# First units of five products begun in the tails of the stages ahead, with four changes of order, in a two-block transformer kernel on one core

## The chip, the core and the metric

The kernel runs on 1 core of a Trainium2 chip as one program. The metric is the device time of one execution in microseconds, from all inputs in device memory to the output there. TensorE (PE) multiplies, VectorE (DVE) and ScalarE (ACT) do the elementwise work, GpSimd (POOL) adds some squares and moves rows, and SyncE (SP) issues the loads.

## The reference, cut to what matters

All of it is fp32, for 512 tokens (plus 256 context tokens in layer 0), width 1024. Two layers of a first block are followed by a second block.

```
def first_block(...):
    for l in range(2):
        ...
        h = h + mx[2] * (yx @ w_out[l])
        h = h + mx[5] * conv_ffn(modulate(rmsnorm(h, norm2_g[l]), mx[3], mx[4]), w_up[l], conv_w[l], conv_b[l], w_down[l])
        ...
    return rmsnorm(h, final_g)

def conv_ffn(h, w_up, conv_w, conv_b, w_down):      # 1024 -> 2 x 2816 -> 1024
    u = h @ w_up
    ...
    return (jax.nn.silu(a) * b) @ w_down
```

The second block normalises the result twice (`final_g`, then `mix_g`), multiplies by `w_in_2`, mixes (latent attention of 8 heads and a "hyena" long convolution with filters computed in the kernel), multiplies by an output matrix, attends to 256 memory tokens with 4 heads of 256 (`w_mq`, `w_mkv`, `w_mo`) and ends in a mixture of 32 experts.

```
def _mem_xattn(hx, hm, w_mq, w_mkv, w_mo):
    q = (hx @ w_mq).reshape(B, S, MEM_HEADS, MEM_HEAD_DIM)
    k, v = jnp.split(hm @ w_mkv, 2, axis=-1)
    ...
    return o @ w_mo
```

## The kernel before, in words

**Stages.** The program is a chain of stages (`with self.stage()`). Each gives every engine a hand-written list of work, with semaphores between the lists. At the end of a stage all engines wait for each other; the profile shows that wait as PEq L784.

**Products in three passes.** A large product (`project`) is made of units: one unit is 128 output rows (a PSUM area), summed over 8 or 22 tiles of 128 input rows. Both operands are split in a high part (rounded, made by ACT, L824, L505 or L608) and a low part (value minus high, made by DVE, L859, L509 or L612). One tile costs three matmuls: high weight by low input, high by high, low by high. A unit of 8 tiles is 24 matmuls, all at L953.

**Weight strips.** Weights come in strips of up to 2048 columns through a ring of 3 slots (`ring`). A strip must be split before PE uses it; its high part goes to one of two areas in turn, so strip s+2 can be split only when PE is done with strip s. `split_order` sets the order of the splits on ACT and DVE alike: first strip 0 (unless the stage ahead has split it, `following_strip` or `split_ahead`), then the tiles that are not ready, then for each unit the strips whose area is free, the norm work (`deferred.on_vector`, `on_scalar`, at unit 0) and the eviction of the unit (`take`). With `early=k` strip 1 is split ahead of tile k; without it, strip 1 comes behind all tiles. `tiles_ahead` says how many tiles the stage ahead has split already.

**The places that the change touches**, in order of time:
1. Down projection of layer 0 (`ffn_down`, no tile ahead): 22 tiles of 768 tokens, two strips of 1408 columns for a unit, strip 1 from tile 11 on.
2. Down projection of layer 1 (9 tiles ahead, 512 tokens). SP first loads the inputs of the hyena filters (`load_hyena_inputs`), and PE stops ahead of unit 1 for them (`FilterFeatures.on_tensor`, L466).
3. `second_projection`, behind `hyena_filters`: 16 units of 8 tiles, 5 tiles ahead (`PAIRED_AHEAD`). Units 0 and 1 use strip 0, units 2 and 3 strip 1, units 4 and 5 strip 2. `PairNorm` adds squares on ACT (L523) and DVE (L547), PE sums them over partitions (L533, in `before`), DVE and ACT form the two inverse roots (L549 to L555), and only then DVE evicts units 0 and 1 (L2291) and splits strip 2.
4. `latent_attention`: 32 steps u (a head's quarter): scores (L1081), maximum (L1149), exponential (L1196), scaling (L1155, L1156), transposition (L1123), copy (L1234), and every 8 steps the values (L1092). At u = 4 ACT splits two whole strips of the next product and at u = 5 DVE does (`high_ahead`, `low_ahead`). Its last sum of squares is L1071.
5. `mixed_projection`: 16 half units. Three of its tiles come from the hyena part and are ready early.
6. `memory_attention`'s product: 24 units of 256 and 512 columns, `MemoryNorm`, 8 memory tiles ahead.
7. The memory attention itself: 16 steps with the same loop, two strips split at u = 4 and 5; copies of values are L1169.
8. `output_projection` behind it: 8 units, 6 of 8 tiles ahead.

## Time and profile before

| | us |
|---|---|
| median of 3 runs | 2773.83 |
| lowest, highest | 2773.24, 2775.17 |
| the profiled execution, its own time | 2779.62 |
| span of its instructions | 2777.8 |
| PE busy in it | 2487.8 (90%) |
| DVE busy | 1375.2 (50%) |
| ACT busy | 868.5 (31%) |
| mean granted TensorE clock | 0.949 |

The profiled execution is one run with the profiler on. Its span starts at the first instruction, and all stretches below are in microseconds of that span. A granted clock of 1.00 is 2.4 GHz and 0.50 is 1.2 GHz; a value between them is a stretch that has some of both.

### The profile page before, as it was taken

How to read it: one execution, taken by the hardware profiler on the slowest of the kernel's cores; microseconds unless marked ns; L12 is line 12 of the kernel's file. 1: busy time of each engine (PE TensorE's matmuls, PEld its weight loads, DVE VectorE, ACT ScalarE, POOL GpSimd, SP SyncE). 2: the span in 40 equal slices, each digit the busy share in tenths (PEclk: the TensorE clock that was granted, in tenths of full speed). 3: DMA queues.
4: the chain of work that ended last, by engine and by line, in shares of the span. 5: the costliest groups of instructions: out<-in, count | busy, mean ns of one | idle time of the engine just before them, and what ended most of it. 6: DMA issues, size and time to landing. Idle time of an engine off the chain costs nothing. (4 is left out here: it accounts for less than half of the span.)

```text
span 2777.8 us, 34833 instructions
## 1 busy us (share of the span) xinstructions
PE 2487.8 (90%) x14602; PEld 1933.5 (70%) x14602; DVE 1375.2 (50%) x2185; ACT 868.5 (31%) x1385; POOL 251.7 (9%) x183
## 2 busy tenths in 40 slices
PE   7997988999998998997889999998977889898976
PEld 5885657888887787995669998764733368573322
DVE  4324554566667214325647777347565645423213
ACT  3222433332324113223444334233424642311001
POOL 0002520000000000003500000000042020011112
PEclk9998989999999999997989999999988999988999
DMA  5114731111111112115612223320201013348997
GB/s 240 61 54 106 269 128 46 46 61 61 63 69 38 53 63 82 61 69 142 224 46 92 92 92 117 111 82 31 87 0 54 0 61 137 121 188 326 421 421 292
DMA packets 58555, 326.88 MB, mean 118 GB/s; under 512 B 8157, under 2 KB 14429, under 8 KB 26461
## 3 DMA queue, kind: packets, MB, share of 16 engines
q1 hardware_dynamic: 45358, 302.76, 29.4%
q0 software_dynamic: 5696, 12.59, 1.2%
q10 hardware_dynamic: 7344, 9.28, 1.0%
q8 instruction: 117, 1.92, 0.3%
q14 instruction: 40, 0.33, 0.0%
HBM read 317.26 MB, written 12.58 MB: 119 GB/s over the span
## 5 line engine op out<-in xcount | busy, mean ns | idle before, releaser
L953 PE MATMUL ps<-work_rounded,ring_rounded 128*128 128x512 f32 (+1 forms) x2016 | 537.0, 354 | 19.1 <-DVE work_rounded L397 10.6
L953 PE MATMUL ps<-xn_rounded,ring_rounded 128*128 128x512 f32 (+2 forms) x2304 | 541.8, 347 | 0.0
L2003 PE MATMUL ps<-xn_rounded,ring_rounded 128*128 128x258 f32 (+2 forms) x2816 | 535.1, 312 | 0.0
L2003 PEld LDWEIGHTS ps<-xn_rounded,ring_rounded 128*128 128x128 f32 x2816 | 414.6, 191 | 31.2
L953 PEld LDWEIGHTS ps<-xn_rounded,ring_rounded 128*128 128x128 f32 x2304 | 373.4, 191 | 57.6 <-issue 0.2
L953 PEld LDWEIGHTS ps<-work_rounded,ring_rounded 128*128 128x128 f32 x2016 | 336.5, 192 | 76.3 <-DVE work_rounded L397 11.8
L953 PE MATMUL ps<-big_rounded,ring_rounded 128*128 128x512 f32 (+1 forms) x1200 | 326.3, 364 | 45.0 <-DVE big_rounded L859 25.0
L859 DVE TENSOR_TENSOR ring_rounded<-ring,ring_rounded 128x2048 fp32r<-128x2048 f32 (+2 forms) x94 | 189.1, 2015 | 266.5 <-ACT ring_rounded L824 266.5
L2003 PE MATMUL ps<-work_rounded,ring_rounded 128*128 128x256 f32 (+1 forms) x1232 | 280.2, 309 | 9.0 <-PEq L784 4.8
L953 PEld LDWEIGHTS ps<-big_rounded,ring_rounded 128*128 128x128 f32 x1200 | 203.4, 196 | 84.8 <-DVE ring_rounded L859 21.4
L824 ACT ACTIVATE ring_rounded<-ring 128x2048 fp32r<-128x2048 f32 (+2 forms) x94 | 158.2, 1687 | 314.7 <-PE ps L953 298.3
L2003 PEld LDWEIGHTS ps<-work_rounded,ring_rounded 128*128 128x128 f32 x1232 | 191.9, 191 | 21.5 <-issue 10.6
L2052 DVE TENSOR_TENSOR ring_rounded<-ring,ring_rounded 128x1024 fp32r<-128x1024 f32 x84 | 103.0, 1226 | 171.4 <-ACT ring_rounded L2017 171.4
L2017 ACT ACTIVATE ring_rounded<-ring 128x1024 fp32r<-128x1024 f32 x84 | 89.0, 1060 | 205.8 <-PE ps L2003 205.8
L2022 ACT ACTIVATE work<-work,small 128x512 f32<-128x512 f32 (+1 forms) x132 | 81.5, 649 | 203.0 <-DVE work L2059 203.0
L1313 ACT ACTIVATE big<-big,small 128x512 f32<-128x512 f32 (+1 forms) x81 | 47.0, 624 | 254.0 <-DVE big L1309 154.0
L1303 DVE COPY small<-ps 128x2 f32<-128x2 f32 x46 | 7.3, 159 | 176.9 <-PE ps L953 176.6
L3320 PE MATMUL ps<-big,work 128*64 128x512 f32 x352 | 80.4, 604 | 15.1 <-DMA big<-in_experts 13.8
L1339 POOL MEMSET work<- 128x792 f32 x2 | 1.5, 758 | 1015.4 <-DMA work<-in_pool 1015.4
L2070 DVE SCALAR_TENSOR_TENSOR work<-work,vec 128x769 f32<-128x769 f32 (+1 forms) x88 | 78.0, 887 | 3.1
L2069 DVE SCALAR_TENSOR_TENSOR work<-work,vec 128x769 f32<-128x769 f32 (+1 forms) x88 | 78.0, 887 | 3.1
L3343 ACT ACTIVATE work<-ps,small 128x256 f32<-128x256 f32 x16 | 7.6, 476 | 221.3 <-PE ps L3320 221.3
(420 smaller groups left out, 3125.4 us busy)
## 6 DMA issues: line engine op xcount, KB each, us to landing
ring<-in_stream SPq DMA_DIRECT2D x141, 1024.0 KB, 4.8
big<-in_experts SPq DMA_DIRECT2D x44, 1024.0 KB, 26.0
ring<-in_stream SPq DMA_DIRECT2D x32, 704.0 KB, 4.0
ring<-in_experts SPq DMA_DIRECT2D x22, 1024.0 KB, 27.3
xn<-in_experts SPq DMA_DIRECT2D x15, 1024.0 KB, 28.4
work<-in_experts SPq DMA_DIRECT2D x15, 1024.0 KB, 28.7
big<-in_first_modulation SPq DMA_DIRECT2D x8, 1024.0 KB, 14.1
work<-in_bias ACTq DMA_DIRECT2D x24, 256.0 KB, 3.9
```

Source lines behind the costliest of these rows:

```text
L824: return act.activation(self.rounded(high), value, ACT.Copy)
L859: return dve.tensor_tensor(self.rounded(value), value, self.rounded(high).bitcast(F32), ALU.subtract)
L953: mm = pe.matmul(out[:, a - u.first:b - u.first], lhs, rhs, start=j == 0 and n == 0 and not u.onto, stop=j == terms - 1 and n == len(passe ...
L1313: act.activation(px[:, m, a:z], px[:, m, a:z], ACT.Identity, bias=bias[:, m, s:s + 1])
L2003: mm = pe.matmul(out[:, a:b], ws[:, k, :], x[k][:, a - base:b - base], start=k == 0 and n == 0, stop=k == KT - 1 and n == 2)
L2017: act.activation(high_w[c], half(i, c)[0], ACT.Copy).then_inc(strip_high.up(), 1)
L2022: ins = act.activation(u[:, i % 2, c, o:o + b - a], u[:, i % 2, c, o:o + b - a], ACT.Identity, bias=bias[:, i % 2, c, s:s + 1])
L2052: dve.tensor_tensor(low_part, value, high_w[c].bitcast(F32), ALU.subtract).then_inc(strip_low.up(), 1)
L2069: settle(dve, dve.scalar_tensor_tensor(out=cc, in0=uu[:, 0:n], scalar=cw(0, t), in1=cc, op0=ALU.mult, op1=ALU.add), vstep)
L2070: dve.scalar_tensor_tensor(out=cc, in0=uu[:, 2:2 + n], scalar=cw(2, t), in1=cc, op0=ALU.mult, op1=ALU.add).then_inc(convolved.up(), 1)
L3320: mm = pe.matmul(b.bank(2)[r, :], self.rows_t[:, k, r], self.gu[s][:, k, :], start=k == 0, stop=k == KT - 1)
L3343: act.activation(self.silu_t, b.bank(2)[:, 0:256], ACT.Silu, scale=b.slot_scale[:, 0, n:n + 1]).then_inc(self.silued, 1)
```

## The change

Four changes of order:
- `PairNorm.before`: PE sums the squares ahead of unit 4 instead of unit 2 (place 3).
- In both attentions the two whole-strip splits become four half-strip splits, on ACT at u = 4, 6, 8, 10 and on DVE at u = 5, 7, 9, 11 (places 4 and 7).
- `ffn_down` gets `early=8` in layer 0 and `early=10` in layer 1 (places 1 and 2).
- The last two tiles of the memory attention's output are split at the end of the attention instead of at the start of the output projection (place 8).

And `begin_unit`: in the tails of the stages ahead, PE issues the first matmuls of the next product. These are 9 tiles of unit 0 (27 matmuls) at place 2, 5 tiles (15) at place 3, 3 tiles of units 0 to 3 (36) at place 5, 7 tiles of 256 columns (21) at place 6, and 6 tiles of units 0 and 1 (36) at place 8. `project` leaves them out then (`begun`). No matmul is added or removed.

```
     def before(self, pe, i):
-        if i == 2:
+        if i == 4:
             pe.wait_ge(b.sig("squares_added").sem, b.sig("squares_added").at(2 * KT - 2))
...
+    def begin_unit(self, pe, out, strip, weight, sources):
+        slot = self.ring[:, strip % RING * STRIP:strip % RING * STRIP + WIDTH[strip]]
+        high_w, low_w = [self.rounded(self.high_of(strip))], [self.rounded(slot)]
+        for j, (low, high) in enumerate(sources):
+            for n, (w, x) in enumerate(((high_w, low), (high_w, high), (low_w, high))):
+                pe.matmul(out, weight(w, j), self.rounded(x), start=j == 0 and n == 0, stop=False)
...
-                    for j, tile in enumerate(u.tiles):
+                    for j, tile in list(enumerate(u.tiles))[begun.get(i, 0):]:
...
+                if begin:
+                    begin(pe)
...
                 values(heads - 1)
+                if begin:
+                    pe.wait_ge(exped.sem, exped.at(units))
+                    begin(pe, 0)
                 if normed_pairs:
                     sum_pair(heads // 2 - 1)
+                if begin:
+                    begin(pe, 1)
...
-                    if u == 5:
-                        self.low_ahead(dve, views)
...
+                    if u in (5, 7, 9, 11):
+                        halves_low((u - 5) // 2)
+                    next_lows(u)
                 store(heads - 1)
+                next_lows(units)
...
-                    if u == 4:
-                        self.high_ahead(act, views)
+                    if u in (4, 6, 8, 10):
+                        halves_high((u - 4) // 2)
+                    next_highs(u)
...
+                if tiles_ahead:
+                    pe.wait_ge(next_low.sem, next_low.at(tiles_ahead + 1))
+                    self.begin_unit(pe, self.ps[:, 0:width], len(self.freed_at), self.down_weight, down_sources[0:tiles_ahead])
...
-        self.project(units, 2 * KT, finish, banks_each=2, sources=sources, tiles_ahead=tiles_ahead,
+        self.project(units, 2 * KT, finish, banks_each=2, sources=sources, tiles_ahead=tiles_ahead, early=10 if last else 8, begun={0: tiles_ahead},
...
+                pe.wait_ge(next_low.sem, next_low.at(PAIRED_AHEAD))
+                pe.wait_ge(taken.sem, taken.at(5))
+                self.begin_unit(pe, self.bank(0), len(self.freed_at), halves(0), norm.rooms[0:PAIRED_AHEAD])
...
-        self.project(units, 4, finish, sources=rooms, deferred=OutputNorm(self, rooms, w[:, 7168:7680]), add=square, gpsimd=add_squares,
-                     following_strip=True, after=after, tiles_ahead=4)
+        self.project(units, 4, finish, sources=rooms, deferred=OutputNorm(self, rooms, w[:, 7168:7680]), add=square, gpsimd=add_squares,
+                     following_strip=True, after=after, tiles_ahead=4, begin=begin, begun={m: 3 for m in range(4)})
...
-        self.project(units, 12, finish, sources=norm.rooms, deferred=norm, early=KT, tiles_ahead=KT)
+        self.project(units, 12, finish, sources=norm.rooms, deferred=norm, early=KT, tiles_ahead=KT, begun={0: KT - 1})
...
-            next_tiles=[(6 + 4 * (m // 2), 2 * (m // 2) + 2, o[:, m, :], self.output_high[m]) for m in range(6)])
+            next_tiles=[(6 + 4 * (m // 2) if m < 6 else 16, 2 * (m // 2) + 2, o[:, m, :], self.output_high[m]) for m in range(KT)], begin=begin)
...
-                               tiles_ahead=6, rooms=self.output_high)
+                               tiles_ahead=KT, rooms=self.output_high, begun={0: 6, 1: 6})
```

How it moves instructions at three of the places. First DVE at place 1, from the start of layer 0's down projection (`big_rounded` is a tile's low part, `ring_rounded` a strip's; a row with x8 stands for eight of them). Before:

```order
L972 UNCONDITIONAL_BRANCH [waits barrier_Pool_Activation_PE_DVE_SP_release]
L859 TENSOR_TENSOR ring_rounded<-ring,ring_rounded 128x1408 [waits strip_high]
L859 TENSOR_TENSOR big_rounded<-big,xn_rounded 128x768 [waits tile_high] x8
L859 TENSOR_TENSOR big_rounded<-big,work_rounded 128x768 [waits tile_high] x14
L859 TENSOR_TENSOR ring_rounded<-ring,ring_rounded 128x1408 [waits strip_high] x2
L2121 SCALAR_TENSOR_TENSOR h<-ps,mods,h 128x512 [waits product_done]
```

With the change:

```order
L984 UNCONDITIONAL_BRANCH [waits barrier_Pool_Activation_PE_DVE_SP_release]
L859 TENSOR_TENSOR ring_rounded<-ring,ring_rounded 128x1408 [waits strip_high]
L859 TENSOR_TENSOR big_rounded<-big,xn_rounded 128x768 [waits tile_high] x8
L859 TENSOR_TENSOR ring_rounded<-ring,ring_rounded 128x1408 [waits strip_high]
L859 TENSOR_TENSOR big_rounded<-big,work_rounded 128x768 [waits tile_high] x14
L859 TENSOR_TENSOR ring_rounded<-ring,ring_rounded 128x1408 [waits strip_high]
L2164 SCALAR_TENSOR_TENSOR h<-ps,mods,h 128x512 [waits product_done]
```

Strip 1 moved from behind tile 21 to ahead of tile 8.

Next PE at place 3, around the sum of squares L533. Before, with the last matmuls of unit 1 ahead of it and the first of unit 2 behind it:

```order
L953 MATMUL ps<-work_rounded,ring_rounded 128x512
L953 MATMUL ps<-xn_rounded,ring_rounded 128x512 x2
L533 MATMUL ps<-xn,base 128x512 [waits squares_added]
L533 MATMUL ps<-xn,base 128x512
L953 MATMUL ps<-work_rounded,ring_rounded 128x512 [waits strip_low]
```

With the change; 96x512 is unit 3, and the `strip_low` behind the sum is that of strip 2:

```order
L963 MATMUL ps<-work_rounded,ring_rounded 96x512
L963 MATMUL ps<-xn_rounded,ring_rounded 96x512 x2
L533 MATMUL ps<-xn,base 128x512 [waits squares_added]
L533 MATMUL ps<-xn,base 128x512
L963 MATMUL ps<-work_rounded,ring_rounded 128x512 [waits strip_low]
```

The sum moved behind two more units. DVE's order at the same place is that of before (the eviction, L2291 before, is now L2337):

```order
L547 TENSOR_TENSOR xn<-xn 128x512 [waits squares_added,squared] x12
L549 TENSOR_SCALAR work<-ps 128x512 [waits summed]
L550 TENSOR_SCALAR xn<-work 128x512 [waits varied]
L551 SCALAR_TENSOR_TENSOR xn<-ps,xn 128x512 [waits vector_step]
L553 RECIPROCAL xn<-xn 128x512 [waits rooted,varied]
L555 RECIPROCAL work<-work 128x512 [waits rooted,vector_step]
L2337 TENSOR_TENSOR big<-ps,xn 128x512 [waits product_done,vector_step]
L2337 TENSOR_TENSOR big<-ps,xn 128x512 [waits product_done]
L859 TENSOR_TENSOR ring_rounded<-ring,ring_rounded 128x2048 [waits strip_high]
```

Nothing moved there: `summed` is what PE's L533 sends, and the last row splits strip 2.

Last DVE at place 4, at steps 5 to 7 of the latent attention. Before:

```order
L1156 TENSOR_SCALAR work<-work,small 128x512 [waits vector_step]
L1149 TENSOR_REDUCE small<-ps 128x1 [waits scored]
L1150 TENSOR_SCALAR small<-small 128x1 [waits vector_step]
L859 TENSOR_TENSOR ring_rounded<-ring,ring_rounded 128x2048 [waits strip_high] x2
L1155 RECIPROCAL small<-small 128x1 [waits exponentials]
L1156 TENSOR_SCALAR work<-work,small 128x512 [waits vector_step]
```

With the change:

```order
L1168 TENSOR_SCALAR small<-small 128x1 [waits vector_step]
L859 TENSOR_TENSOR ring_rounded<-ring,ring_rounded 128x1024 [waits strip_high]
L1173 RECIPROCAL small<-small 128x1 [waits exponentials]
L1174 TENSOR_SCALAR work<-work,small 128x512 [waits vector_step]
L1167 TENSOR_REDUCE small<-ps 128x1 [waits scored]
L1168 TENSOR_SCALAR small<-small 128x1 [waits vector_step]
L1173 RECIPROCAL small<-small 128x1 [waits exponentials]
L1174 TENSOR_SCALAR work<-work,small 128x512 [waits vector_step]
L1167 TENSOR_REDUCE small<-ps 128x1 [waits scored]
L1168 TENSOR_SCALAR small<-small 128x1 [waits vector_step]
L859 TENSOR_TENSOR ring_rounded<-ring,ring_rounded 128x1024 [waits strip_high]
L1173 RECIPROCAL small<-small 128x1 [waits exponentials]
```

Two whole strips in a row became one half every second step.

## Rows read from the trace of the kernel before

**Rows 1.** The page, part 1: busy time of each engine, share, instructions.

```profile
PE 2487.8 (90%) x14602; PEld 1933.5 (70%) x14602; DVE 1375.2 (50%) x2185; ACT 868.5 (31%) x1385; POOL 251.7 (9%) x183
```

**Rows 2.** PE's waits, whole span: total us, times, longest us.

```profile
PE ps L953 <- DVE big_rounded L859: 25.0, 3, 12.1
PE ps L1123 <- DVE work L1156: 24.9, 21, 6.0
PE ps L953 <- PEq L784: 15.1, 5, 6.0
```

**Rows 3.** PE by stretches: start:end length, busy (x matmuls), clock, DMA share, GB/s.

```profile
912.74:918.37 5.63, 5.63 (x17) 0.50 0.00 0
...
1718.54:1724.58 6.04, 0.01 (x1) 0.66 0.34 119
...
2155.50:2158.58 3.08, 2.93 (x12) 1.00 0.00 0
2167.51:2171.97 4.46, 4.46 (x13) 0.60 0.00 0
2234.43:2238.09 3.66, 1.13 (x3) 1.00 0.00 0
2238.09:2283.11 45.02, 45.02 (x192) 1.00 0.20 71
2301.32:2304.15 2.83, 0.00 (x0) 1.00 0.64 197
2304.15:2307.59 3.44, 3.44 (x16) 0.50 0.35 143
2418.28:2419.42 1.14, 1.14 (x6) 1.00 0.00 0
2406.42:2408.60 2.18, 2.18 (x6) 0.50 0.00 0
2432.99:2434.11 1.12, 0.00 (x1) 1.00 0.00 0
```

**Rows 4.** The page, part 5: splits of 1024 columns; busy us, mean ns.

```profile
L2052 DVE TENSOR_TENSOR ring_rounded<-ring,ring_rounded 128x1024 fp32r<-128x1024 f32 x84 | 103.0, 1226 | 171.4 <-ACT ring_rounded L2017 171.4
L2017 ACT ACTIVATE ring_rounded<-ring 128x1024 fp32r<-128x1024 f32 x84 | 89.0, 1060 | 205.8 <-PE ps L2003 205.8
```

**Rows 5.** Timeline at place 1: start, length, instruction, [idle before <- releaser].

```profile
898.91 12.25 DVE L859 TENSOR_TENSOR big_rounded<-big,work_rounded 128x768 fp32r<-128x768 f32 x14
...
903.74 0.51 PE L953 MATMUL ps<-big_rounded,ring_rounded 128*128 128x512 f32 x2
...
912.74 1.01 PE L953 MATMUL ps<-big_rounded,ring_rounded 128*128 128x512 f32 x2 [5.70 <-DVE ring_rounded L859]
```

**Rows 6.** Timeline at place 2: the splits, and the stop for the hyena inputs.

```profile
1725.21 7.32 DVE L859 TENSOR_TENSOR big_rounded<-big,xn_rounded 128x512 fp32r<-128x512 f32 x12 [1.02 <-ACT xn_rounded L824]
...
1742.92 1.07 PE L466 MATMUL ps<-work,vec 33*64 33x512 f32 x2
```

**Rows 7.** DMA traffic of 1724 to 1744, in 40 slices of 0.5 us.

```profile
GB/s 0 0 12 153 351 243 360 246 246 197 229 295 475 377 492 754 98 737 246 590 442 344 541 246 590 197 737 246 541 101 438 383 383 101 23 34 11 0 0 34
```

**Rows 8.** Timeline at place 3: bank 0 read, the sum, the chain behind it.

```profile
1901.63 0.68 DVE L2248 COPY big<-ps 1x512 f32<-1x512 f32 x1 [3.18 <-PE ps L2209]
...
1920.23 1.98 PE L533 MATMUL ps<-xn,base 128*128 128x512 f32 x4 [2.30 <-DVE xn L547]
...
1935.00 2.29 DVE L859 TENSOR_TENSOR ring_rounded<-ring,ring_rounded 128x2048 fp32r<-128x2048 f32 x1 [2.03 <-ACT ring_rounded L824]
...
1937.35 0.79 PE L953 MATMUL ps<-work_rounded,ring_rounded 128*128 128x512 f32 x1 [4.02 <-DVE ring_rounded L859]
```

**Rows 9.** Timeline at places 4 and 7: the whole-strip splits and what PE waited.

```profile
2162.37 4.50 DVE L859 TENSOR_TENSOR ring_rounded<-ring,ring_rounded 128x2048 fp32r<-128x2048 f32 x2 [1.35 <-ACT ring_rounded L824]
...
2406.42 0.69 PE L1123 MATMUL ps<-base,work 128*128 128x128 f32 x2 [5.68 <-DVE work L1156]
...
2418.28 0.44 PE L1123 MATMUL ps<-base,work 128*128 128x128 f32 x2 [1.28 <-DVE work L1156]
```

More of the change, by code:

```diff
@@ L878, in project @@
     def project(self, units, strips, finish, sources, banks_each=1, prefetch=None, deferred=None, add=None, gpsimd=None,
-                early=None, following_strip=False, loads=None, following_halves=False, after=None, beside=None, tiles_ahead=0):
+                early=None, following_strip=False, loads=None, following_halves=False, after=None, beside=None, tiles_ahead=0,
+                begun={}, begin=None):
         first = len(self.freed_at)
@@ L1197, in exponentials, with next_highs, halves_high @@
                                    accum_out=stat[:, 2, b:b + 1]).then_inc(exped.up(), 1)
+                def next_highs(u):
+                    for at_unit, outputs, value, high in next_tiles:
+                        if u == at_unit:
+                            act.wait_ge(stored.sem, stored.at(outputs))
+                            self.split_high(act, value, high).then_inc(next_high.up(), 1)
+                def halves_high(part):
+                    for n, value, high in views[part // 2:part // 2 + 1]:
+                        r = slice(part % 2 * 1024, part % 2 * 1024 + value.shape[1] // 2)
+                        self.strip(act, n)
+                        self.split_high(act, value[:, r], high[:, r]).then_inc(strip_high.up(), 1)
                 def square_pair(p):
@@ L2115, in ffn_down @@
         g, segments = self.g, self.gates(l, 5, need_ctx)
-        units = [Unit([2 * m, 2 * m + 1], lambda w, j: w[j // 11].rearrange("p (k c) -> p k c", k=FT // 2)[:, j % 11, :], range(FT), P, width)
-                 for m in range(KT)]
+        units = [Unit([2 * m, 2 * m + 1], self.down_weight, range(FT), P, width) for m in range(KT)]
         def finish(eng, i, ps):
@@ L2631, in rows, with begin @@
             return slice(64 * (h % 2), 64 * (h % 2) + 64)
+        next_low, strip = self.sig("next_low"), len(self.freed_at)
+        def begin(pe, part):
+            if part == 0:
+                pe.wait_ge(next_low.sem, next_low.at(4))
+            for m in (2 * part, 2 * part + 1):
+                self.begin_unit(pe, self.bank(m), strip, self.half_strip(m), [(mix[:, 4 + i, :], self.hyena_high()[i]) for i in range(3)])
         self.attention(
@@ L2722, in finish, with begin @@
             return dve.tensor_tensor(dst[i], ps, memory_rstd if i < KT else stream_rstd, ALU.mult)
-        self.project(units, 12, finish, sources=norm.rooms, deferred=norm, early=KT, tiles_ahead=KT)
+        self.project(units, 12, finish, sources=norm.rooms, deferred=norm, early=KT, tiles_ahead=KT, begun={0: KT - 1})
         self.output_high = tiles_in(S, w[:, 3072:7168])
         self.sparse = SparseExperts(self)
+        next_low, strip = self.sig("next_low"), len(self.freed_at)
+        def begin(pe, part):
+            if part == 0:
+                pe.wait_ge(next_low.sem, next_low.at(6))
+            self.begin_unit(pe, self.bank(2 * part), strip, halves(part), [(o[:, m, :], self.output_high[m]) for m in range(6)])
         self.attention(
```

56 lines of the change are left out of this document (34 added, 22 removed).

## The prediction

> **What bounds the kernel now.** I read the busy times first: PE is busy 90% of the span [rows 1], so what can be won is PE's idle time and the time in which it runs at 1.2 GHz. PE's waits come next [rows 2]: the three longest entries add up to 65 us, and most single waits are of 1 to 12 us at a stage's border or inside an attention. Then I went to each place that the change touches and asked which engine ends the wait there. Three prices recur. At 2.4 GHz 192 matmuls of 512 columns take 45.02 us [rows 3], so 0.2345 us each, 0.70 us for a tile and 5.63 us for a unit of 8 tiles. Behind the waits of 5.7 us at place 1 and 2.83 us at place 6 PE came back at 1.2 GHz, for 5.63 and 3.44 us, both at clock 0.50 [rows 3]; such a stretch costs half its length. And a split of 1024 columns takes DVE 1.23 us and ACT 1.06 [rows 4].
>
> **Place 1, down projection of layer 0 (early=8).** PE waits 5.70 us at 912.74 for strip 1 [rows 5], since DVE split 22 tiles first, the last 14 of them in 12.25 us. Now strip 1 comes ahead of tile 8. It has 1408 columns, so it takes at most 1.7 us. That delays tile 8, the first of the 14 in [rows 5], from 898.91 + 0.88 = 899.8 to 901.5. PE needs it at 903.74 [rows 5], so 2.2 us of cover are left, and the later tiles come every 0.88 us, quicker than PE uses them (three matmuls of 512 columns and three of 256, so 1.05 us). The wait goes whole, and with it the 5.63 us at 1.2 GHz behind it [rows 3], worth 2.8. Next late is nothing: DVE is then ahead of PE. Sum: 5.7 + 2.8 = **+8.5 us** (between 5.7, if the clock fell all the same, and 8.5).
>
> **Place 2, down projection of layer 1 (9 tiles begun, early=10).** PE idled 6.04 us at the border [rows 3] while DVE ended the convolution. The 27 matmuls take 6.3 us at 2.4 GHz and fill that. PE then is the last at the border, by some 0.7 us. Behind it tile 9 comes first, strip 1 (1.7 us) next, then tiles 10 to 21 at DVE's 0.61 us each (7.32 us for 12 [rows 6]), faster than PE's 0.70. PE would end unit 0 near 1738, against 1742.92, where L466 starts [rows 6]. But L466 waits for the hyena inputs, four loads of 4.9 MB together, that SP issues at the border. Traffic stays high until 1740.5 [rows 7]; the last 0.7 MB are a strip queued behind them, so they land between 1739.3 and 1740.9, and 0.7 us later with the border. PE goes on between 1740.0 and 1741.6. The transfer, hidden before, takes half of the gain. Sum: 1742.9 - 1740.5 = **+2.4 us** (1.3 to 2.9). A stretch at 1.2 GHz in unit 0 would be lost in the same wait.
>
> **Place 3, second projection (15 begun, sum ahead of unit 4).** This is where I expect a loss. The wait of 4.02 us at 1937.35 ends with DVE's split of strip 2 [rows 8], and that split stands on DVE behind everything that follows the sum: three steps, two roots on ACT, two reciprocals, the evictions of units 0 and 1, then ACT's high part. From the start of the sum (1920.23) to PE's next unit (1937.35) the chain takes 17.1 us [rows 8]. Before, PE did units 2 and 3 (11.3 us) beside it and waited 4.02. With the change units 2 and 3 stand ahead of the sum, nothing of PE's is left beside the chain, and unit 4 needs its end. When does the sum start? The 15 begun matmuls (3.5 us) can start when DVE has read bank 0, at 1902.3 [rows 8], and end at 1905.9; the border moves some 1.2 us later, tiles 5 to 7 follow until about 1910.0, three units (16.9) until 1926.9. The chain ends at 1926.9 + 17.1 = 1944.0, against 1937.35: **-6.7 us** (-5 to -10; the upper end if PE runs the units ahead of the sum at 1.2 GHz for two stretches of 3.4 us). The wait of 2.30 us in [rows 8] is gone, and one of some 15 us comes. Queued behind DVE's wait for the sum are the evictions and strip 2. The begun matmuls alone bring nothing here: with the sum ahead of unit 2 it would still wait for the squares, which start at the border.
>
> **Places 4 and 7, halves in the attentions.** In the latent attention PE waited 6.0 us while DVE split two strips in 4.50 us [rows 9], and then ran two steps in 4.46 us that take 3.08 elsewhere [rows 3]: 5.9 more than usual, plus 1.4 for the clock, 7.3. Now each half is 1.23 us on DVE and 1.06 on ACT. A step is a loop through DVE, ACT and PE with about no slack (PE is busy 2.93 of the 3.08 us of two steps [rows 3], and waits for DVE's scaling each time, 21 waits in [rows 2]), so DVE's 4 x 1.23 = 4.9 all shows. The first half also waits for ACT (0.5 us), and the second stands ahead of a copy that PE needs (0.6). That is 6.0 to 6.3, so **+1.0 us** (-1.8, if ACT's four add in full, 9.1, to +7.3, if all is hidden). In the memory attention PE waited 5.68 us [rows 9], of which 1.28 is the wait at the same step of the next head [rows 9], and one step took 2.18 us for 1.14 [rows 3]: 5.4 in all. The same halves cost 4.9 plus about 1.1, where tiles are split at the same steps: **-0.6 us** (-3.7 to +5.4).
> The first row is 4.50 us for two whole strips, and four halves are 4.9. The Trainium skill, in Perfetto Trace Analysis, Optimizing Scalar/DVE Operations, says that breaking up instructions may allow work to be completed sooner where these engines aren't saturated but cause bubbles on others. By that rule the halves vanish in the idle time; the rows on the loop speak against it, and the case is a rival below.
>
> **Place 5, tail of the latent attention (36 begun).** PE idled 3.66 - 1.13 = 2.5 us [rows 3] around the last sum. The 36 matmuls (8.4 us) cover that; what stays is the border itself, about 0.4 us. DVE's and ACT's work of the next stage starts 6 us later, but PE has 60 of its first 96 matmuls left (14 us); DVE needs about as long for strip 2. **+2.0 us** (1.3 to 2.2).
>
> **Place 6, memory products (21 begun).** They fill idle time ahead of the border, but PE waits again at 2301.32 for 2.83 us [rows 3], and that wait ends with DVE's list (strip 1, eight tiles, three reciprocals, two evictions, strip 2), which starts at the border whatever PE has done. Nothing is won. The wait grows to some 7 us, and the 3.44 us at 1.2 GHz behind it [rows 3] may get longer: **-0.4 us** (-1.7 to 0).
>
> **Place 8, output projection (36 begun, two tiles split earlier).** PE idled 1.12 us [rows 3] and now about 0.4: **+0.7 us** (0.3 to 0.7). The two splits lie beside the begun matmuls.
>
> **Sum.** 8.5 + 2.4 - 6.7 + 1.0 - 0.6 + 2.0 - 0.4 + 0.7 = +6.9 us. The profiled execution took 2779.62 us, 1.8 more than its span and 5.8 more than the median of the three runs. 2779.6 - 6.9 = 2772.7, and less 5.8 it is 2766.9: I say **2767 us**. The loads of the experts at the end start from PE's progress and shift with it.
>
> **Rivals.**
> (a) Slower. At both attentions ACT's half adds to DVE's, and the repeated gaps keep the clock at 1.2 GHz through steps 5 to 12. Each then costs 9.1 us, plus 8 steps at 4.46 for 3.08 per two (5.5) in one and some 4 in the other: 14.6 and 13.1 us against 7.3 and 5.4. That is 15 us worse, and 0.4 less gain: 2767 + 15.4 = 2782; with only one of the two, near 2775. It decides from the granted clock there falling to 0.5 for more than 5 us. For it speaks the 0.60 at 2167.51 [rows 3]; against it that each gap would be under 2.6 us, and that the clock is 1.00 right behind the 1.28 us wait in the memory attention [rows 3].
> (b) The late sum costs nothing, because strip 2 is not behind the chain as I read it. Then place 3 wins the 2.30 us instead of losing 6.7: 2758. Against it: the row ahead of 1937.35 is that split.
> (c) The halves vanish in idle time, by the rule above: 12.7 us won for my 0.4, so 2754.7. DVE has idle time only while PE runs the values.
> (d) The begun matmuls and early strips move work and little else: place 1 gives only 5.7, place 2 1.3, place 3 costs 9: 6.9 - 2.8 - 1.1 - 2.3 = 0.7, so 2773.
>
> **How the numbers follow.** My forecast, 2763 to 2770, has a chance of 0.52; (d) and what lies between, 2770 to 2775, 0.30; (a) 0.08; (b) 0.06; (c) 0.04. The range reaches from 2760 to 2774. A measurement can tell about 0.2%, 5.5 us, from no change. The border of 2768.3 cuts my forecast: faster 0.37 of its 0.52, plus (b), (c) and a part of (d) (0.09), is 0.56; slower is most of (a) and a little of (d), 0.07; the rest, 0.37, is within.
>
> **What the changed profile would show.** Right: at place 1 no wait of PE between 907 and 919 and clock 1.00 there. At place 2 PE busy through the border and a new wait of about 2 us ahead of L466. At place 3 L533 without a wait of its own, and behind it PE waiting some 15 us for L859. In the attentions four waits of 1 to 2.5 us for one of 6. At place 6 a wait of about 7 us for 2.8. Wrong: a wait under 8 us behind L533, a clock of 0.50 through the attentions, or strip 1 still late at place 1.

## The result, and the profile after

The changed kernel is slower. Its four runs took 2781.85, 2790.98, 2791.21 and 2790.30 us (median 2790.64), against a median of 2774.5 for before beside them; the ratio is 1.0045, with a 95% interval of 1.0033 to 1.0057. Measured again on another chip (11 runs, below) it was 1.0035 (1.0020 to 1.0051). These ratios, here and below, are estimates over all runs and not quotients of the medians. The forecast was 2767 us.

The profiled execution of the changed kernel is the one of 2781.85 us. Its busy times (the page, part 1) differ from [rows 1] by hardly anything, since no product was added:

```profile
PE 2486.1 (89%) x14602; PEld 1927.9 (69%) x14602; DVE 1376.2 (50%) x2189; ACT 869.3 (31%) x1389; POOL 252.0 (9%) x183
```

So I cut both traces at the stages' borders. The columns of the view by stretches are start:end, length, PE busy (x matmuls), granted clock, DMA share, GB/s. Before, from the border ahead of the hyena filters' stage (`hyena_filters`, between places 2 and 3), then that stage, place 3, place 4, place 5, place 6, place 7 and place 8:

```profile
1852.12:1853.30 1.18, 0.01 (x1) 1.00 0.35 56
1853.30:1901.59 48.29, 45.60 (x104) 1.00 0.05 21
1901.59:2006.46 104.87, 94.93 (x388) 0.95 0.18 63
2148.04:2234.43 86.39, 68.80 (x262) 0.92 0.05 19
2234.43:2283.11 48.68, 46.15 (x194) 1.00 0.19 65
2283.11:2384.86 101.75, 95.68 (x585) 0.97 0.36 125
2385.98:2432.99 47.01, 35.24 (x128) 0.93 0.32 133
2432.99:2479.13 46.14, 45.02 (x193) 1.00 0.33 134
```

The same view of the changed kernel: first place 1 without any wait, then the same eight stretches, with the low clock inside the filters' stage as a row of its own:

```profile
891.59:1078.26 186.67, 186.67 (x1056) 0.99 0.17 62
...
1835.17:1836.35 1.18, 0.01 (x1) 1.00 0.41 76
1836.35:1896.08 59.73, 58.86 (x104) 0.77 0.04 16
1838.47:1865.78 27.31, 27.31 (x33) 0.50 0.03 11
...
1896.08:2008.78 112.70, 94.77 (x388) 0.91 0.16 59
2150.14:2235.97 85.83, 70.75 (x263) 0.92 0.05 20
2235.97:2282.40 46.43, 46.02 (x197) 1.00 0.19 68
2282.40:2385.30 102.90, 95.30 (x585) 0.95 0.35 123
2386.41:2437.07 50.66, 38.41 (x129) 0.90 0.30 123
2437.07:2482.47 45.40, 44.99 (x192) 1.00 0.34 137
```

A stretch that begins with matmuls issued ahead holds them: 2282.40 has the 21 of place 6. All stretches of the two profiled spans, in us (minus is time won):

| stretch | before | after | difference | forecast |
|---|---|---|---|---|
| start to end of layer 0's up projection | 880.98 | 879.52 | -1.5 | 0 |
| place 1, with its border | 207.31 | 198.74 | -8.6 | -8.5 |
| from there to the end of layer 1's up projection | 630.25 | 624.99 | -5.3 | 0 |
| place 2, up to L466 | 24.38 | 22.68 | -1.7 | -2.4 |
| rest of that down projection | 109.20 | 109.25 | 0 | 0 |
| **hyena filters' stage** | **48.29** | **59.73** | **+11.4** | **0** |
| place 3 | 104.87 | 112.70 | +7.8 | +6.7 |
| layout stage | 141.58 | 141.36 | -0.2 | 0 |
| place 4 | 86.39 | 85.83 | -0.6 | -1.0 |
| place 5 | 48.69 | 46.43 | -2.3 | -2.0 |
| place 6 | 101.75 | 102.89 | +1.1 | +0.4 |
| place 7 | 47.01 | 50.65 | +3.6 | +0.6 |
| place 8 | 46.14 | 45.41 | -0.7 | -0.7 |
| routing and experts | 298.67 | 297.50 | -1.2 | 0 |

They add up to +2.2 before rounding, which is 2780.0 - 2777.8; two border waits, 1.2 us each in both kernels, are left out. The eight places that the change touches won 1.2 us together, for 6.9 in the forecast. The filters' stage lost 11.4, and all other stages won 8.1 without being touched. The largest entry stands in a stage of which the change moves only the start. There PE came out of the same border wait of 1.18 us in both kernels. The timeline (start, length, instruction, [idle before <- releaser]) shows how the products went on, before:

```profile
1853.30 9.25 PE L2192 MATMUL ps<-work,big 65*128 65x512 f32 x21 [1.18 <-PEq L784]
```

and with the change:

```profile
1836.35 14.46 PE L2235 MATMUL ps<-work,big 65*128 65x512 f32 x19 [1.18 <-PEq L784]
```

21 records took 9.25 us, then 19 took 14.46. Before, the clock stayed at 1.00 (2.4 GHz). With the change it fell to 0.50 (1.2 GHz) 2.1 us behind the start and stayed there for 27.31 us, in all of which PE was busy. Ahead of the fall PE had worked from 1725.93 to 1835.17 with no gap over 0.3 us and had waited 1.18 us.

The timeline of place 3 with the change, in answer to [rows 8]: the tile that the begun unit waits for, the sum, PE's next unit, and DVE's split of strip 2 that releases it.

```profile
1902.60 0.51 PE L963 MATMUL ps<-work_rounded,ring_rounded 128*128 128x512 f32 x1 [1.95 <-DVE work_rounded L509]
...
1923.00 1.88 PE L533 MATMUL ps<-xn,base 128*128 128x512 f32 x4
...
1937.65 2.29 DVE L859 TENSOR_TENSOR ring_rounded<-ring,ring_rounded 128x2048 fp32r<-128x2048 f32 x1 [2.03 <-ACT ring_rounded L824]
...
1940.00 0.80 PE L963 MATMUL ps<-work_rounded,ring_rounded 128*128 128x512 f32 x1 [15.12 <-DVE ring_rounded L859]
```

The timeline of place 2, in answer to [rows 6]: two short waits for tiles, and the stop for the hyena inputs.

```profile
1711.19 0.50 PE L963 MATMUL ps<-big_rounded,ring_rounded 128*128 128x512 f32 x1 [1.79 <-DVE big_rounded L859]
...
1713.99 0.80 PE L963 MATMUL ps<-big_rounded,ring_rounded 128*128 128x512 f32 x1 [1.84 <-DVE big_rounded L859]
...
1725.93 1.07 PE L466 MATMUL ps<-work,vec 33*64 33x512 f32 x2 [0.98 <-DMA work<-in_dft]
```

### The profile page after: what moved, and what is told of

Read it like the earlier page. It is cut to its first block and busy times, and to the rows that moved or that the text cites. A ratio compares the mean times of both kernels' runs of the same rounds, so it can differ in the third digit from the quotient of the medians.

```text
span 2780.0 us, 34845 instructions
## 1 busy us (share of the span) xinstructions
PE 2486.1 (89%) x14602; PEld 1927.9 (69%) x14602; DVE 1376.2 (50%) x2189; ACT 869.3 (31%) x1389; POOL 252.0 (9%) x183
## 5 line engine op out<-in xcount | busy, mean ns | idle before, releaser
L963 PE MATMUL ps<-work_rounded,ring_rounded 128*128 128x512 f32 (+2 forms) x1963 | 517.6, 352 | 30.3 <-DVE ring_rounded L859 15.1
L963 PE MATMUL ps<-xn_rounded,ring_rounded 128*128 128x512 f32 (+1 forms) x2294 | 541.6, 348 | 0.0
L963 PEld LDWEIGHTS ps<-work_rounded,ring_rounded 128*128 128x128 f32 x1963 | 325.0, 191 | 83.7 <-DVE ring_rounded L859 15.9
L963 PE MATMUL ps<-big_rounded,ring_rounded 128*128 128x512 f32 (+1 forms) x1128 | 304.5, 360 | 37.1 <-DVE big_rounded L859 28.6
L859 DVE TENSOR_TENSOR ring_rounded<-ring,ring_rounded 128x2048 fp32r<-128x2048 f32 (+3 forms) x98 | 190.0, 1939 | 255.2 <-ACT ring_rounded L824 255.2
L824 ACT ACTIVATE ring_rounded<-ring 128x2048 fp32r<-128x2048 f32 (+3 forms) x98 | 159.2, 1625 | 298.1 <-PE ps L963 273.0
L963 PEld LDWEIGHTS ps<-big_rounded,ring_rounded 128*128 128x128 f32 x1128 | 188.8, 194 | 73.6 <-DVE ring_rounded L859 19.4
L2041 PEld LDWEIGHTS ps<-work_rounded,ring_rounded 128*128 128x128 f32 x1232 | 191.3, 190 | 21.5 <-issue 10.6
```

Source lines behind the costliest of these rows:

```text
L824: return act.activation(self.rounded(high), value, ACT.Copy)
L859: return dve.tensor_tensor(self.rounded(value), value, self.rounded(high).bitcast(F32), ALU.subtract)
L963: mm = pe.matmul(out[:, a - u.first:b - u.first], lhs, rhs, start=j == 0 and n == 0 and not u.onto, stop=j == terms - 1 and n == len(passe ...
L2041: mm = pe.matmul(out[:, a:b], ws[:, k, :], x[k][:, a - base:b - base], start=k == 0 and n == 0, stop=k == KT - 1 and n == 2)
```

## The experiments

My first theory, **A**: in the filters' stage the clock falls or stays depending on where in time the stage's start lies, so any shift of some us can cost or give 11.4 us. Its rival, **B**: the changed kernel's own work (the begun matmuls, the early strips) brings the fall. Kernels that have the same median of before beside them ran on one chip. "Long" is a filters' stage of 59.7 us, "short" one of 48.3; its length is counted from the end of the border wait.

| kernel | filters' stage in the trace | median us (lowest to highest, runs) | before beside it | ratio, 95% interval |
|---|---|---|---|---|
| e1_again | 59.72 | 2787.5 (2771.8 to 2794.7, 11) | 2776.2 | 1.0035, 1.0020 to 1.0051 |
| e2_sum2 | 59.73 | 2782.6 (2778.3 to 2785.8, 8) | 2776.2 | 1.0022, 1.0011 to 1.0032 |
| e3_early | 48.29 | 2769.1 (2764.2 to 2781.7, 12) | 2776.2 | 0.9981, 0.9970 to 0.9993 |
| e5_after8 | 48.30 | 2778.3 (2769.7 to 2781.9, 11) | 2776.2 | 1.0004, 0.9995 to 1.0013 |
| e6_before8 | 48.28 | 2790.3 (2778.3 to 2794.8, 12) | 2777.1 | 1.0035, 1.0021 to 1.0049 |
| e7_whole | 59.72 | 2780.7 (2768.1 to 2785.5, 11) | 2777.1 | 1.0001, 0.9987 to 1.0014 |
| e8_few | 59.73 | 2775.7 (2761.1 to 2782.2, 12) | 2777.1 | 0.9985, 0.9970 to 1.0000 |
| e9_head8 | 49.58 (with 1.9 more work) | 2777.1 (2771.2 to 2789.5, 12) | 2777.1 | 1.0004, 0.9990 to 1.0018 |
| e4_late | 48.29 | 2787.5 (2785.0 to 2788.8, 5) | 2778.1 | 1.0038, 1.0025 to 1.0051 |
| e10_few_tail4 | 48.29 | 2762.4 (2760.1 to 2766.6, 6) | 2778.1 | 0.9951, 0.9939 to 0.9963 |
| e11_few_tail8 | 48.28 | 2763.5 (2759.4 to 2770.3, 6) | 2778.1 | 0.9957, 0.9945 to 0.9969 |
| e12_few_head4 | 48.64 (with 0.9 more work) | 2765.2 (2763.5 to 2771.0, 6) | 2778.1 | 0.9961, 0.9949 to 0.9974 |

**e1_again: the changed kernel, unaltered.**

> The changed kernel once more, unaltered. Theory A (the clock decides, by where a stage starts): the stage of the hyena filters again takes some 59.7 us against 48.3 before, with some 27 us of it at clock 0.50, and the second projection takes some 112.7 us against 104.9; if the clock falls at other places in this run, its span differs from 2780.0 by just those stretches. Theory B (the begun matmuls themselves are dear): each begun block is longer than 0.2345 us a matmul, and the loss is there in every run, whatever the clock.

By stretches: the filters' stage, the low clock in it, place 3, the layout stage, place 4:

```profile
1838.89:1898.61 59.72, 58.86 (x104) 0.77 0.04 16
1840.48:1867.79 27.31, 27.31 (x33) 0.50 0.05 21
1898.61:2011.10 112.49, 94.56 (x389) 0.92 0.17 59
2011.10:2155.27 144.17, 104.89 (x301) 0.87 0.08 26
2155.27:2244.76 89.49, 74.61 (x263) 0.87 0.05 19
```

The loss in the filters' stage and that at place 3 are back to 0.2 us. That a begun matmul is dear in itself, the rival on record here, is out: place 5 with its 36 ran its 197 matmuls in 46.02 us, 0.234 each. This span is 2789.0 us, 9.0 more than the first, and so like the three other runs there. 2.8 of the 9.0 lie in the layout stage (144.17 for 141.36), 3.7 at place 4 (89.49 for 85.83) and 2.5 ahead of the filters' stage. At place 4 the clock's mean is lower, 0.87 for 0.92. So the first profiled execution (2781.85) lies near the low end of this kernel's runs, and that of before (2779.62) near the high end of its own, which lie from 2772.5 to 2780.2 here. That is why the two traces differ by 2.2 us and the medians by 11 to 16.

**e2_sum2 and e4_late: the late sum, taken out and done alone.** e2 is the changed kernel with

```
-        if i == 4:
+        if i == 2:
```

and e4 is the kernel before with the reverse edit.

> The changed kernel with the sum of squares back ahead of unit 2. Theory (late sum is dear): the wait of 15.12 us behind the sum is gone and one of some 3 to 5 us is back; the second projection is 6 to 8 us shorter than in the changed kernel, so the kernel 5 to 8 us faster than it (some 2783 against 2790 for timed runs). Rival (the wait only moves, since strip 2 is late for another reason): within 2 us of the changed kernel.

> The kernel before with the sum of squares ahead of unit 4 instead of unit 2, nothing else. By the prediction on record: L533 has no wait of its own, PE waits some 13 to 14 us behind it for strip 2, and the second projection takes some 110.5 us for 104.9, so 5.6 us slower (the begun matmuls' part of the 6.7 left out). Rival (the late sum is cheap, and the changed kernel's longer stage comes from the begun matmuls): within 1 us of 104.9. All stages ahead are those of before, so the filters' stage should stay at 48.3 us.

Place 3 by stretches, in e2 and then in e4, and e4's sum and next unit in the timeline:

```profile
1899.19:2007.21 108.02, 97.30 (x388) 0.94 0.17 61
```

```profile
1893.75:2006.61 112.86, 94.13 (x388) 0.92 0.16 59
```

```profile
1921.18 1.88 PE L533 MATMUL ps<-xn,base 128*128 128x512 f32 x4
1938.18 0.80 PE L953 MATMUL ps<-work_rounded,ring_rounded 128*128 128x512 f32 x1 [15.12 <-DVE ring_rounded L859]
```

The late sum alone makes place 3 8.0 us longer (112.86 for 104.87); I had expected 5.6. The wait of 15.12 us behind it is the changed kernel's to the hundredth. Taking it back won 4.5 us in the stage (108.02 for 112.49) and 5.0 in the median; 6 to 8 were expected in the stage. Most of the 3.5 us between 8.0 and 4.5 goes with the 15 begun matmuls: with them place 3 is 108.02 with the sum ahead of unit 2, without them (e8) 105.22. The squares on ACT and DVE start only at the border, and the begun matmuls push the border back. In e2 the sum itself also ran at 1.2 GHz, 3.54 us for the 1.98 of [rows 8].

**e3_early: before with the two early strips alone.**

```
-        self.project(units, 2 * KT, finish, banks_each=2, sources=sources, tiles_ahead=tiles_ahead,
+        self.project(units, 2 * KT, finish, banks_each=2, sources=sources, tiles_ahead=tiles_ahead, early=10 if last else 8,
```

> The kernel before with strip 1 ahead of tile 8 and of tile 10 in the two down projections, nothing else. Theory: 8.5 us won at place 1, as in the changed kernel (down projection of layer 0 from 195.2 us to 186.7), and about nothing at place 2 as long as the hyena inputs are waited for there; so 8 us faster than before, give or take what the clock does in the stages behind, whose starts all move by 8.5 us. Theory A says that a moved start can lose up to 11 us in the filters' stage at clock 0.50 (or not); rival: the clock in the filters' stage is 1.00 as before, since nothing is begun ahead of it, and the whole 8.5 us stay.

Place 1 took 198.60 us for 207.31, the filters' stage was short, and the median is 7.2 us lower. This one argument gives a faster kernel than the whole change does. Two of its 12 runs took 2779.0 and 2781.7 us, 10 to 13 more than the median. They have no trace, so whether the filters' stage was long in them isn't shown.

**e5_after8, e6_before8, e13 to e15: the start moved, nothing else.** Ahead of the last unit of layer 1's down projection PE gets n more matmuls, whose result isn't used: n is 8 in e5 (on the changed kernel) and in e6, e14 and e15 (on the kernel before), and 6 in e13 (on the kernel before).

```
+        if i == 7:
+            extra = b.rounded(b.down_sources(1, S)[0][0][1])
+            for _ in range(n):
+                pe.matmul(b.bank(7), extra[:, 0:P], extra, start=True, stop=True)
```

> The changed kernel with eight more matmuls of 128x512 (their result is not used) ahead of the last unit of layer 1's down projection: 1.9 us of more work. It moves the start of the filters' stage by 1.9 us and changes nothing else in what comes before it. Theory A (the clock falls there by where the border lies in time): the stage keeps clock 1.00 and takes some 48.3 us, so the kernel is 11.4 - 1.9 = 9.5 us faster than the changed kernel in the profiled run. Rival (it falls because of what the changed kernel does ahead of it, the begun matmuls or the earlier strips): the stage takes 59.7 us again and the kernel is 1.9 us slower.

> The kernel before with eight more matmuls of 128x512 (result unused) ahead of the last unit of layer 1's down projection, 1.9 us of work. Theory A (the start's place in time decides what the clock does in the filters' stage): the same edit that took 11.4 us away from that stage in the changed kernel now adds 11.4 us to it (59.7 us for 48.3, some 27 us at clock 0.50), and the kernel is some 13 us slower than before. Rival B (dense work just ahead of the stage keeps the clock up, wherever the start lies): the stage stays at 48.3 us and the kernel is 1.9 us slower.

> The kernel before with six more matmuls of 128x512 (result unused, 1.4 us) ahead of the last unit of layer 1's down projection. Theory A: the shift by 1.4 us puts the start of the filters' stage where the changed kernel's lies, the stage takes 59.7 us at clock 0.50 for some 27 us, and the span is some 2790. Rival (the changed kernel's own work is needed for the fall): 48.3 us at 1.00, span some 2779.

> The kernel before with eight more matmuls once more, for a trace of one of its longer runs (8 of 12 were 11 us longer than the other 4). Theory A: a longer run has the filters' stage at 59.7 us and 0.50, a shorter one at 48.3 us and 1.00. Rival: the 11 us of a longer run lie elsewhere.

> As e14_before8_again, a further look at the kernel before with eight more matmuls: a longer run has the filters' stage at 59.7 us, a shorter one at 48.3 us.

The filters' stage of e5, e6, e13 and e15, in this order (e14 took 59.72 us):

```profile
1838.38:1886.68 48.30, 45.60 (x104) 1.00 0.05 21
```

```profile
1851.42:1899.70 48.28, 45.60 (x104) 1.00 0.05 21
```

```profile
1851.04:1910.77 59.73, 58.87 (x104) 0.77 0.04 17
```

```profile
1851.21:1910.94 59.73, 58.86 (x104) 0.77 0.04 17
```

This speaks for A. 1.9 us of extra work make the changed kernel's stage short and the kernel 9.2 us faster (2778.3 for 2787.5, expected 9.5), and the same 1.9 us make the kernel before 13.2 us slower (2790.3 for 2777.1, expected 13). B is out: e13, e14 and e15 have nothing of the change and fall all the same. So is the rival of e6, that dense work just ahead of the border keeps the clock up: e14 and e15 have the eight matmuls there and are long.

A single trace can't carry this, since e6 and e15 are the same program, their border waits end at 1851.42 and 1851.21, and one is short and the other long. The timed runs can. The 12 of e6 lie in two groups with nothing between them: four at 2778.3 to 2779.3 and eight at 2789.2 to 2794.8. e6's own trace, short, is of a run of 2779.06 us; those of e14 and e15, long, are of 2791.6 and 2789.4 (e13's is of 2793.05). So the shift changes how often the stage is long.

The traces also show from where the place of the start has to be counted: not from the start of the span, but from the clock's own changes. In each trace the changes of the granted clock, some 70, lie on a raster, that is, any two are one same distance or a multiple of it apart, to 0.005 us. The border wait ended 1.00 to 1.93 us behind the last point of that raster in the eight long traces. In the seven short ones without extra work behind the border it ended at 0.09 (e3) or at 1.97 (e6) to 3.10 us (before). The edge is sharp: from the clock's last change to the end of the wait e15 has 124.81 us (1726.40 to 1851.21) and is long, e6 has 124.85 (1726.57 to 1851.42) and is short. The expectation of e10 puts the two groups 1.1 us apart, which e6 doesn't bear out. This is A in a sharper form, read from 15 traces; no run was made to test it.

**e7_whole: whole strips in both attentions.** The changed kernel with

```
-                    if u in (5, 7, 9, 11):
-                        halves_low((u - 5) // 2)
+                    if u == 5:
+                        self.low_ahead(dve, views)
...
-                    if u in (4, 6, 8, 10):
-                        halves_high((u - 4) // 2)
+                    if u == 4:
+                        self.high_ahead(act, views)
```

> The changed kernel with the two whole strips split in a row again in both attentions (ACT at step 4, DVE at step 5), all else as changed. Theory by the trace of the changed kernel: the memory attention takes some 47.0 us again instead of 50.65, and the latent attention about the same as with halves, with 2 us to either side for the clock: 2 to 5 us faster than the changed kernel in these two stages. The prediction on record would say: latent attention 1.0 us slower with whole strips, memory attention 0.6 faster, so no difference.

Places 4 and 7 by stretches:

```profile
2151.58:2237.90 86.32, 68.72 (x263) 0.92 0.05 19
2388.19:2435.19 47.00, 35.67 (x129) 0.93 0.32 133
```

The four waits with a half ahead of them in the changed kernel's timeline:

```profile
2403.57 0.44 PE L1136 MATMUL ps<-base,work 128*128 128x128 f32 x2 [2.41 <-DVE work L1174]
...
2408.81 0.69 PE L1136 MATMUL ps<-base,work 128*128 128x128 f32 x2 [2.85 <-DVE work L1174]
...
2418.56 0.56 PE L1136 MATMUL ps<-base,work 128*128 128x128 f32 x2 [2.41 <-DVE work L1174]
...
2424.33 0.44 PE L1136 MATMUL ps<-base,work 128*128 128x128 f32 x2 [1.71 <-DVE work L1174]
```

In the memory attention whole strips are 3.7 us better (47.00 for 50.66), and so in every trace: the twelve with whole strips took 47.00 to 47.04 us, the five with halves 50.60 to 52.28. The four halves make PE wait 2.41 + 2.85 + 2.41 + 1.71 = 9.4 us. The first wait, 2.41, is about 1.23 on DVE plus 1.06 on ACT [rows 4]: both halves stand in the same loop and add. But this isn't where the 3.7 us come from, since the kernel with whole strips waits at the same four steps too (5.68 + 0.24 + 1.27 + 1.29 = 8.5 us in e7). PE's waits for DVE in the whole stage (total us, times, longest) are, with halves, in e7 and before:

```profile
PE ps L1136 <- DVE work L1174: 10.7, 6, 2.9
```

```profile
PE ps L1136 <- DVE work L1174: 9.8, 6, 5.7
```

```profile
PE ps L1123 <- DVE work L1156: 10.2, 6, 5.7
```

0.9 us of the 3.7 are waits. The other 2.7 are PE's busy time, 38.41 us for 35.67 with the same work. The clock was at 0.50 for 10.24 us in three stretches with halves, nearly all of them busy:

```profile
2408.50:2411.91 3.41, 3.10 (x6) 0.50 0.00 0
2418.74:2422.15 3.41, 3.41 (x11) 0.50 0.01 2
2432.39:2435.80 3.41, 3.41 (x5) 0.50 0.00 0
```

In the kernel before it was one stretch, and PE waited through half of it:

```profile
2403.16:2409.99 6.83, 3.57 (x11) 0.50 0.00 0
```

In the latent attention the two forms can't be told apart: five traces with halves lie from 85.8 to 92.6 us, twelve with whole strips from 86.3 to 89.5. The median fell by 7 us against e1, on another chip; I count only the 3.7 as shown.

**e8_few: the change without what lost.** The changed kernel with the sum ahead of unit 2, whole strips, and without `begin_unit` and `begun` at places 3 and 6.

> The changed kernel with the sum ahead of unit 2 again, whole strips in both attentions, and nothing begun at places 3 and 6; what stays are the early strips, the begun matmuls at places 2, 5 and 8 and the two tiles split earlier. Theory (the sum of the terms that gained): 8.5 at place 1, 1.7 at place 2, 2.2 at place 5, 0.7 at place 8, so 13 us under before (some 2762 against 2775), if the clock in the filters' stage stays at 1.00; 11 us more, so 2 under before, if it falls there. Rival (gains at borders are given back by the clock wherever it falls): the timed runs spread over 20 us and their median is within 3 us of the kernel before.

The filters' stage, places 3, 6 and 7:

```profile
1838.61:1898.34 59.73, 58.86 (x104) 0.77 0.05 17
1898.34:2003.56 105.22, 95.44 (x388) 0.95 0.18 63
2281.86:2382.09 100.23, 93.96 (x585) 0.98 0.36 126
2383.20:2430.20 47.00, 35.39 (x129) 0.93 0.32 133
```

Places 3 and 7 are those of before. But the filters' stage was long, so only a little is left of the gain (ratio 0.9985), and the 12 runs lie over 21 us. At place 6 four traces without the begun matmuls took 100.2 (three) and 102.7 us, six with them 101.6 to 102.9, and before 101.75: the clock scatters as much as they cost.

**e9_head8 and e12_few_head4: dense work behind the border.** The same matmuls stand at the start of `hyena_filters` instead, eight on the changed kernel and four on e8.

```
+                extra = self.rounded(self.down_sources(1, S)[0][0][1])
+                for _ in range(n):
+                    pe.matmul(self.bank(7), extra[:, 0:P], extra, start=True, stop=True)
                 for u, (o, t, d) in enumerate(units):
```

> The changed kernel with eight more matmuls of 128x512 (result unused) right behind the start of the filters' stage, ahead of its first product. Theory A' (the clock falls there where the border's idle time comes together with the first products of the filters, which have 65 rows and start in pairs): with 1.9 us of dense work between the two it stays at 1.00 in every run, the stage takes 48.3 + 1.9 = 50.2 us for 59.7, and the timed runs lie closer together than those of the changed kernel (23 us apart) with a median some 9 us lower. Rival (only the shift by 1.9 us counts): the stage falls as often as before, and median and spread stay.

> The reduced change with four such matmuls (0.94 us) behind the start of the filters' stage instead. Theory A' (dense work between the border and the first products of the filters): the stage takes 48.3 + 0.9 = 49.2 us with clock 1.00; median near 2766. Rival: 0.94 us of dense work is too little, the clock falls to 0.50 as in the reduced change, and the kernel is at 2777.

The stage was at 1.00 in both traces (49.58 and 48.64 us from the end of the border wait), and the medians are 10.5 us under e1 and 10.5 under e8, both comparisons across chips. But e9's runs still lie 18 us apart (23 in e1), against what I expected. So something else varies too, or the stage still falls in some; without a trace of its long runs this stays open. These two kernels shift the products as e5 and e11 do, so they don't tell whether the dense work helps or only the shift of the products. One thing they do show: in e12 the border wait ended 1.84 us behind the raster's last point, which is inside the range of the long traces (1.00 to 1.93), and the stage was short. So the place of the wait alone doesn't decide; what runs right behind it counts as well.

**e10_few_tail4 and e11_few_tail8: the version that beats both.** e8 with four or eight matmuls ahead of the last unit, as in e5.

> The reduced change (sum ahead of unit 2, whole strips in the attentions, nothing begun at places 3 and 6) with four more matmuls of 128x512 (result unused, 0.94 us) ahead of the last unit of layer 1's down projection. Theory A (the start's place in time decides): 0.94 us later is enough to keep clock 1.00 in the filters' stage in most runs, since the shifts that kept it lay 1.1 us and more later against the clock's changes than the starts that lost it; so the stage takes 48.3 us and the median is 11.4 - 0.9 less than that of the reduced change in its slower runs, near 2766. Rival (the shift has to be 1.9 us): the stage falls as in the reduced change, 2776.

> The reduced change with eight such matmuls (1.9 us) ahead of the last unit of layer 1's down projection. Theory A: the filters' stage keeps clock 1.00 and takes 48.3 us; median some 2767, 9 us under before. Rival (other stages fall to 1.2 GHz in its place, the sum of such stretches being about constant): median near that of before, 2776.

The filters' stage and place 3 of e10:

```profile
1833.65:1881.94 48.29, 45.60 (x104) 1.00 0.05 21
1881.94:1987.00 105.06, 95.28 (x389) 0.95 0.18 63
```

e11's stage took 48.28 us, so both were short. e10 is 15.7 us faster than before by the medians (2762.4 for 2778.1, ratio 0.9951) and its runs lie within 6.5 us. 0.94 us of shift was enough in these six runs. A matmul whose result nobody uses is no sound way to hold a clock, since any later edit ahead of it moves the start again. It shows what the start's place is worth.

## Why the prediction was wrong, point by point

**The direction.** It fell with a step that the sum put at 0 without a reason. The prediction added up the places and let every stage between them move as it was ("the loads of the experts at the end ... shift with it"). That took for granted that a moved stage keeps its clock. The filters' stage gave 11.4 us away, and layer 1's stages between places 1 and 2 gained 5.3 (they spent 51 us at clock 0.50 for 58 before). Without the 11.4 the profiled execution would have been 2770.4 us, close to the 2772.7 that the sum gave for one, but that is luck: the eight places won 1.2 us for 6.9, and stages that the sum left at 0 won 8.1, most of them ahead of place 2 (5.3 and 1.5). These gains are the clock's scatter in good part: e1's trace of the same program has 2.5 less of them ahead of the filters' stage and 2.8 less in the layout stage. The timed runs say the same. With the stage short in its trace (e5) the changed kernel took 2778.3 us, 2776.4 without the extra 1.9, and before beside it 2776.2. So the fall explains why the change is slower, and the places why it isn't faster without the fall.

The rival on the slower side, (a), has the right kind of mechanism, a stretch at 1.2 GHz, but in the wrong place: I looked for it only where the change adds waits. The largest clock effect was where it adds none.

**Place 1** was right: no wait, 8.6 us won for 8.5. **Place 2** was right in kind, 1.7 for 2.4 (range 1.3 to 2.9): PE ends ahead of the loads and waits for them (0.98 us, forecast about 2). The two tile waits of 1.8 us weren't forecast, and DMA's wait hid them.

**Place 3** was the right loss for the right reason, and a little small: 7.8 for 6.7 (range 5 to 10). The chain from the sum to the next unit took 17.0 us (1923.00 to 1940.00; 17.1 in the forecast). The sum came 26.9 us behind the end of the filters' stage and not 25.3. Missed was the wait of 1.95 us for tile 5 (`work_rounded`, L509): before, PE had five tiles of work at the border while DVE made it. The line "the begun matmuls alone bring nothing here" was too kind; they cost 2.8 us where the sum is early (e2 against e8). Rival (b) is out.

**Places 5 and 8** were right: 2.3 for 2.0 and 0.7 for 0.7. **Place 6** had its forecast wait (6.85 us in the changed trace, about 7 forecast) and cost 1.1 for 0.4, within the range.

**Place 7** is the term that was mis-sized most: +3.6 us for +0.6, at the end of its range (3.7). The step that failed is the clock's part of it. The sum priced the whole strips at 4.4 us of waits and 1.04 at 1.2 GHz, and the halves at 6.0 of waits and nothing at 1.2 GHz. Measured against before, PE's waits for DVE grew by 0.5 us (10.7 for 10.2), less than the 1.6 forecast, and PE's busy time by 3.2 (38.41 for 35.24): the clock fell three times, and PE worked 9.9 us at 1.2 GHz for 3.6, of which half is 3.2. Rival (a) had the right kind of mechanism here, more than 5 us at 0.5, but not the size: for its 9.1 us of waits, and the sum's 6.0, 4.4 + 0.5 = 4.9 were measured. At **place 4**, -0.6 for -1.0 in one trace and +3.1 in the other, the clock's scatter is larger than the term. The rule of the Trainium skill (Perfetto Trace Analysis, Optimizing Scalar/DVE Operations), that breaking up instructions may let work complete sooner, isn't borne out here: at place 7 the waits were 10.7 us for 9.8 in e7 and the stage 3.7 us longer, and rival (c) is out. **Rival (d)** had the idea that little is won, but not the means.

**The range** left out the scatter as well. The kernel before lay within 8 us in 31 runs and within 14 in 35 on another chip, and I took its three runs, 1.9 us apart, for the spread of any kernel with this code. The changed one lay within 23 us.

## What to carry to other kernels

A change that wins at one place moves every later stage, and a stage whose first products follow a short border wait can lose more by the granted clock than the change wins: give such stages a term, and look at them first when the sum and the measurement part. Before blaming the edit, move the stage by a few dummy matmuls on both kernels. Cutting work that stands in a loop without slack didn't shorten the waits (10.7 us for 10.2 at place 7), and its several short waits cost more of the clock than the one long one: read PE's busy time beside its waits. A sum that starts a long chain on other engines belongs as early as its inputs allow, with PE's units behind it.

## What was not expected of the hardware

In the changed kernel's trace, after 109 us of steady work at 2.4 GHz and one wait of 1.18 us, the clock fell to 1.2 GHz for 27.31 us, though PE was busy in all of them. It did so, for as long, in all eight traces with a long stage (59.72 or 59.73 us), and in none of the other nine, with the border waits alike. The two outcomes occur in one and the same program (e6 and e15). What tells them apart in the traces is the place of the border wait among the clock's own changes, to 0.04 us, and in e12 what ran right behind it. Whether it matters that the first products here have 65 rows and are fp32 wasn't separated, and why one kernel's starts fall mostly on one side (31 runs of before within 8 us) and another's on both stays open.
